# DeltaNet scan: where the next step's arguments and seeds stand between the two halves of the join, and the tails half a level later

## What is computed

```
a_mat = jnp.where(strict, jnp.einsum('bhncd,bhnsd->bhncs', kb, k) * decay, 0.0)
lhs = a_mat + jnp.eye(c_, dtype=a_mat.dtype)
rhs = jnp.concatenate([kb * jnp.exp(g_cum)[..., None], v * beta], axis=-1)
wu = lax.linalg.triangular_solve(lhs, rhs, left_side=True, lower=True)
...
v_new = u_i - jnp.einsum('bhcd,bhde->bhce', w_i, s)
s_new = s * jnp.exp(gl_i)[..., None, None] + jnp.einsum('bhcd,bhce->bhde', kt_i, v_new)
...
o_i = jnp.einsum('bhcd,bhde->bhce', qd_i, s) + jnp.einsum('bhcs,bhse->bhce', qk_i, v_new)
```

## Time and profile before

| | |
|---|---|
| median of 3 runs | 3947.25 us (3944.8 to 3965.12) |
| the profiled execution's own time | 3948.46 us |
| its span | 3946.6 us |
| mean granted clock of TensorE over the span | 0.952 |
| busy in the span: PE, DVE, ACT, POOL | 3696.8, 1920.1, 1100.5, 990.2 us |

### The profile page before, as it was taken

How to read it: one execution, slowest core, us unless ns; L and a number is a source line. 1 busy time by engine, 2 the same in 40 slices (tenths; PEclk the granted TensorE clock), 3 DMA queues, 4 the chain that set the end, 5 groups by cost and what they waited for, 6 DMA issues and landing times.

```text
span 3946.6 us, 78512 instructions
## 1 busy us (share of the span) xinstructions
PE 3696.8 (94%) x33918; PEld 3059.9 (78%) x33918; DVE 1920.1 (49%) x3377; ACT 1100.5 (28%) x2490; POOL 990.2 (25%) x731
## 2 busy tenths in 40 slices
PE   6999999888899999999998999999889899999997
PEld 5668888677788888888886668888677678888885
DVE  3455556444555333333357455556354554434445
ACT  3444243343312111011114453252343230001111
POOL 1000100144104333323223000100254043434341
PEclk8999999888799999999999999999797899999998
DMA  4240000100001010101111220000100111111111
GB/s 184 88 170 33 22 23 22 60 4 4 23 33 43 33 43 32 43 32 42 43 41 56 84 108 23 23 12 22 50 4 4 44 42 49 48 49 46 51 45 54
DMA packets 30530, 180.54 MB, mean 46 GB/s; under 512 B 2592, under 2 KB 8224, under 8 KB 15136
## 3 DMA queue, kind: packets, MB, share of 16 engines
q1 hardware_dynamic: 28944, 173.66, 11.8%
q10 hardware_dynamic: 1296, 2.61, 0.2%
HBM read 167.87 MB, written 8.39 MB: 45 GB/s over the span
## 4 chain that ended last, share of the span: by engine, by line
PE 84%; DVE 8%; ACT 5%; issue 2%; POOL 1%; DMA 1%; ACTq 0%; DVEq 0%; POOLq 0%; SPq 0%
PE ps L1401 38%; PE ps L801 9%; PE ps L811 8%; PE ps L836 4%; PE ps L934 4%; PE ps L976 2%; PE ps L1264 2%; PE ps L1273 2%; PE ps L1240 2%; PE ps L1328 1%; PE ps L1301 1%; PE ps L1019 1%; PE ps L1354 1%; PE ps L1041 1%; PE ps L845 1%
## 5 line engine op out<-in xcount | busy, mean ns | idle before, releaser
L1401 PE MATMUL ps<-Yn_parts,ring_parts 128*128 128x512 f32 (+1 forms) x3888 | 799.0, 367 | 2.4 <-DVE Yn_parts L2670 2.1
L1401 PEld LDWEIGHTS ps<-Yn_parts,ring_parts 128*128 128x128 f32 x3888 | 671.3, 189 | 126.7 <-DVE Yn_parts L2670 5.4
L1401 PE MATMUL ps<-temp_parts,ring_parts 128*128 128x512 f32 (+1 forms) x2560 | 726.3, 369 | 5.0 <-DVE Hn_parts L2611 3.6
L2930 POOL TENSOR_TENSOR ring_parts<-ring,consts 128x2048 fp32r<-128x2048 f32 x62 | 286.5, 4621 | 1154.5 <-DMA ring<-in_ff 1154.5
L1401 PEld LDWEIGHTS ps<-temp_parts,ring_parts 128*128 128x128 f32 x2560 | 464.9, 189 | 87.9 <-DVE Hn_parts L2611 4.1
L2558 DVE SCALAR_TENSOR_TENSOR Xn<-ps,mods,Xn 128x256 f32<-128x256 f32 (+1 forms) x364 | 251.8, 692 | 574.7 <-PE ps L1401 504.1
L801 PE MATMUL ps<-ring_parts,Xn_parts 128*128 128x256 f32 x2560 | 504.1, 292 | 24.1 <-DVE Hn_parts L2169 16.2
L1401 PE MATMUL ps<-Hn_parts,ring_parts 128*128 128x512 f32 (+1 forms) x1280 | 471.4, 368 | 0.0
L801 PEld LDWEIGHTS ps<-ring_parts,Xn_parts 128*128 128x128 f32 x2560 | 416.8, 195 | 27.2 <-issue 22.6
L1973 ACT ACTIVATE Yn<-ps 128x256 f32<-128x256 f32 (+1 forms) x160 | 88.6, 554 | 1237.8 <-PE ps L1401 1237.8
L2669 DVE TENSOR_TENSOR Yn<-Yn 128x256 f32<-128x256 f32 (+1 forms) x160 | 182.8, 1143 | 402.6 <-ACT Yn_parts L1975 402.6
(11 more groups left out here) (331 smaller groups left out, 5192.3 us busy)
## 6 DMA issues: line engine op xcount, KB each, us to landing
ring<-in_ff SPq DMA_DIRECT2D x64, 1024.0 KB, 4.7
ring<-in_ada SPq DMA_DIRECT2D x22, 2048.0 KB, 8.8
ring<-in_halves SPq DMA_DIRECT2D x28, 1024.0 KB, 4.8
Xn<-in_x SPq DMA_DIRECT2D x1, 5120.0 KB, 16.7
Hn<-in_ada SPq DMA_DIRECT2D x2, 2048.0 KB, 20.7
Xn<-in_x SPq DMA_DIRECT2D x2, 2048.0 KB, 18.2
kept_x<-Xn SPq DMA_DIRECT2D x4, 1024.0 KB, 4.0
Xn<-kept_x SPq DMA_DIRECT2D x1, 4096.0 KB, 14.8
```

The costliest lines, as they stand in the source:

```text
L1401: m = pe.matmul(ps[:, bank, 0:hi - lo], w[a][:, k, j * P:(j + 1) * P], x[b][:, k, lo:hi], start=(k == 0 and part == 0), stop=(k == k_n - 1 ...
L2930: link(TT(by(half_hi[s]), by(half[s]), spread(ones, 1, HALF // P), ALU.mult))
```

## The change

The list of the plan is written in another order, and what this needs is added:

- `arg` of q = 0 of the step after the next moves from behind `b` to between `a` and `b`; its `exp`, `gram` and `at` move into the first two levels of the next step. Both `seed`s and `start`s of the next step stand ahead of `b` on TensorE, and the first level stands directly behind `b`.
- `x1`, `off`, `x2` and `tail` of the step before move half a level later. `qkd` and `at` of q = 1 move to the last level. GpSimd's part of `reach` is an entry of its own, `rest`, behind `atm`.
- `lower` exists twice, for even and odd steps, and lies in `Yn`. `start` waits for the `a` of two steps ago.
- `b` writes to bank 0 (before: bank 3), behind the seed of the next step in the same bank, and starts no new sum there except in the last step. The wait for the copied inverse goes from `y` of level 1, q = 1, to `u` of level 1, q = 0.

The number of products, copies and additions is the same.

```diff
-            plan += one("gsum", 1, 0) + part("arg", 1, 0) + one("exp", 1, 0)
-            plan += both("start", 0) + both("seed", 0) + one("gram", 1, 0) + part("at", 1, 0) + both("kept", 0) + both("kt", 0)
+            plan += one("gsum", 1, 0) + part("arg", 1, 0)
+            plan += both("start", 0) + both("seed", 0) + both("kept", 0) + both("kt", 0)
...
-                plan += y(1) + late("x1", 0) + late("x1", 1) + soon("qkd", 0) + soon("mask", 0)
-                plan += u(1) + late("off", 0) + late("off", 1) + soon("pk", 0)
-                plan += y(2) + late("x2", 0) + soon("gsum", 1) + late("x2", 1) + soon("atm", 0)
-                plan += u(2) + part("arg", s_ + 1, 1) + late("tail", 0) + soon("exp", 1)
-                plan += y(3) + soon("gram", 1) + late("tail", 1)
-                plan += u(3) + part("at", s_ + 1, 1)
-                plan += y(4) + soon("qkd", 1) + late("acc", 0) + late("acc", 1) + one("reach", s_, 0)
-                plan += u(4) + soon("pk", 1) + one("reach", s_, 1) + soon("atm", 1)
-                plan += [("a", s_, 0, 0)] + both("wide", s_) + soon("start", 0) + then("gsum", 0)
-                plan += [("b", s_, 0, 0)] + soon("seed", 0) + soon("start", 1) + soon("mask", 1) + soon("seed", 1)
-                plan += part("arg", s_ + 2, 0) + then("exp", 0) + then("gram", 0) + part("at", s_ + 2, 0)
+                plan += y(1) + soon("exp", 0) + soon("gram", 0)
+                plan += u(1) + late("x1", 0) + late("x1", 1) + part("at", s_ + 1, 0)
+                plan += y(2) + late("off", 0) + late("off", 1) + soon("qkd", 0) + soon("mask", 0)
+                plan += u(2) + soon("pk", 0) + late("x2", 0) + soon("gsum", 1) + late("x2", 1) + soon("atm", 0)
+                plan += part("arg", s_ + 1, 1, (0, 1)) + y(3) + part("arg", s_ + 1, 1, (2, 3)) + late("tail", 0)
+                plan += u(3) + soon("exp", 1) + soon("gram", 1) + late("tail", 1) + late("acc", 0) + late("acc", 1)
+                plan += y(4) + part("at", s_ + 1, 1) + one("reach", s_, 0) + soon("start", 0)
+                plan += u(4) + soon("qkd", 1) + soon("pk", 1) + soon("atm", 1) + one("rest", s_, 0) + one("reach", s_, 1) + one("rest", s_, 1)
+                plan += [("a", s_, 0, 0)] + then("gsum", 0) + soon("seed", 0) + soon("start", 1) + both("wide", s_) + part("arg", s_ + 2, 0)
+                plan += soon("seed", 1) + [("b", s_, 0, 0)] + soon("mask", 1)
...
-                            if s_ and q == 1:
-                                pe.wait_ge(sems["u_inv0"], nth("u_inv0", 2 * s_))
-                                pe.wait_ge(sems["u_inv1"], nth("u_inv1", s_))
...
+                        if lv == 1 and q == 0 and s_:
+                            pe.wait_ge(sems["u_inv0"], nth("u_inv0", 2 * s_))
+                            pe.wait_ge(sems["u_inv1"], nth("u_inv1", s_))
...
+                        if s_ + 1 < NT:
+                            pe.wait_ge(sems["u_umm0"], nth("u_umm0", 5 * s_ + 6))
...
-                                    m = pe.matmul(ps[near, 3, of32(h, P)], sc[0]["step"][far, h, :], sc[q_]["upper"][far, h, :],
-                                                  start=True, stop=True, skip_group_check=True)
+                                    m = pe.matmul(ps[near, 0, of32(h, P)], sc[0]["step"][far, h, :], sc[q_]["upper"][far, h, :],
+                                                  start=(s_ + 1 == NT), stop=True, skip_group_check=True)
...
-                        if s_:
-                            dve.wait_ge(sems["u_lmm0"], nth("u_lmm0", 2 * s_ - 1))
-                        dve.transpose(flat(b["lower"]), b["atm"][s_ % 2][:, 0, :]).then_inc(sems[f"u_start{q}"], tally(f"u_start{q}"))
+                        if s_ >= 2:
+                            dve.wait_ge(sems["u_lmm0"], nth("u_lmm0", 2 * s_ - 3))
+                        dve.transpose(flat(b["lower"][s_ % 2]), b["atm"][s_ % 2][:, 0, :]).then_inc(sems[f"u_start{q}"], tally(f"u_start{q}"))
...
-                    if what == "reach":
+                    if what == "rest":
                         pool.wait_ge(sems[f"u_tv{q}"], nth(f"u_tv{q}", 4 * s_ + 1))
```

More of the change, by code:

```diff
@@ L401, in build @@
             b = {}
-            for n_ in ("lower", "upper", "step", "pk"):
+            for n_ in ("upper", "step", "pk"):
                 b[n_], r0_ = cut(ringf, r0_, H, 32)
+            b["lower"] = []
+            for _ in range(2):
+                half_, y0 = cut(Yn, y0, H, 32)
+                b["lower"].append(half_)
             b["inv"], r0_ = cut(ringf, r0_, H, 64)
@@ L1251, in dn_scan @@
                         for r in blocks32:
-                            m = pe.matmul(pair[r, 0:P], ident[r, r], b["lower"][r].rearrange("p h c -> p (h c)"), start=True, stop=False, skip_group_check=True)
+                            m = pe.matmul(pair[r, 0:P], ident[r, r], b["lower"][s_ % 2][r].rearrange("p h c -> p (h c)"), start=True, stop=False, skip_group_check=True)
                         m.then_inc(sems[f"u_umm{q}"], tally(f"u_umm{q}"))
@@ L1263, in dn_scan @@
                             for r in blocks32:
-                                m = pe.matmul(prod[r, of32(h)], atm[r, lv, of32(h)], b["lower"][r, h, :], start=True, stop=True, skip_group_check=True)
+                                m = pe.matmul(prod[r, of32(h)], atm[r, lv, of32(h)], b["lower"][s_ % 2][r, h, :], start=True, stop=True, skip_group_check=True)
                         m.then_inc(sems[f"u_ymm{q}"], tally(f"u_ymm{q}"))
@@ L1281, in dn_scan @@
                                     m = pe.matmul(ps[far, 2, of32(h, P)], sc[q_]["at"][s_ % kept_back(q_)][near, h, far],
-                                                  sc[q_]["lower"][near, h, :], start=True, stop=True, skip_group_check=True)
+                                                  sc[q_]["lower"][s_ % 2][near, h, :], start=True, stop=True, skip_group_check=True)
                         m.then_inc(sems["u_lmm0"], tally("u_lmm0"))
@@ L1872, in dn_scan @@
                         act.wait_ge(sems[f"u_umm{q}"], nth(f"u_umm{q}", 5 * s_ + lv + 1))
-                        A(flat(b["lower"]), ps[:, q, 0:P], ACT.Copy).then_inc(sems[f"u_lower{q}"], tally(f"u_lower{q}"))
+                        A(flat(b["lower"][s_ % 2]), ps[:, q, 0:P], ACT.Copy).then_inc(sems[f"u_lower{q}"], tally(f"u_lower{q}"))
                     if what == "a":
@@ L1883, in dn_scan @@
                                 near, far = blocks32[n_], blocks32[f_ % 2]
-                                m = A(sc[q_]["inv"][near, :, far], hd32(ps[near, 3, P:2 * P]), ACT.Copy)
+                                m = A(sc[q_]["inv"][near, :, far], hd32(ps[near, 0, P:2 * P]), ACT.Copy)
                             m.then_inc(sems[f"u_inv{q_}"], tally(f"u_inv{q_}"))
@@ L2495, in dn_scan @@
                         dve.wait_ge(sems[f"u_staged{q}"], nth(f"u_staged{q}", 2 * s_ + 1))
-                        if s_:
-                            dve.wait_ge(sems["u_lmm0"], nth("u_lmm0", 2 * s_ - 1))
-                        dve.transpose(flat(b["lower"]), b["atm"][s_ % 2][:, 0, :]).then_inc(sems[f"u_start{q}"], tally(f"u_start{q}"))
+                        if s_ >= 2:
+                            dve.wait_ge(sems["u_lmm0"], nth("u_lmm0", 2 * s_ - 3))
+                        dve.transpose(flat(b["lower"][s_ % 2]), b["atm"][s_ % 2][:, 0, :]).then_inc(sems[f"u_start{q}"], tally(f"u_start{q}"))
                     if what == "u":
                         dve.wait_ge(sems[f"u_lower{q}"], nth(f"u_lower{q}", 4 * s_ + lv))
-                        dve.transpose(flat(b["upper"]), flat(b["lower"])).then_inc(sems[f"u_upper{q}"], tally(f"u_upper{q}"))
+                        dve.transpose(flat(b["upper"]), flat(b["lower"][s_ % 2])).then_inc(sems[f"u_upper{q}"], tally(f"u_upper{q}"))
                     if what == "wide":
```

## The result

The changed kernel takes 3980.65 us (median of 12 runs, 3959.6 to 3999.98), beside 3954.56 us of the kernel before on the same chip (12 runs, 3944.71 to 3972.41). The ratio is 1.0058, 95% interval 1.0036 to 1.0079: it is slower, by 26 us between the medians and 23 us by the ratio, and outside of the predicted range.

The account below looks back on a forecast made before the run. TensorE's join waits and half clock were taken to bound the scans. Join -27.7, pk 1 +24.8, pk 0 +7.2, issue -5.4 (together -1) and clock -23 made -24 on 3948.46: 3924.5, as a median 3923; range 3890 to 3965 us.

Parts of the forecast that it names:

- Join, -27.7: From a to gram: TensorE's waits at seeds and gram go, 1.54 us a step, -27.7 us over 18 steps.
- pk 1, +24.8: Before pk of q = 1: TensorE newly waits for VectorE's qkd, 1.7 us at full clock, 0.1 at half; +24.8 us.
- pk 0, +7.2: Before pk of q = 0: TensorE waits for the later qkd, 0.5 us at full clock, none at half; +7.2 us.
- Moved at no cost: Later x1, off, x2, tails, and GpSimd's rest: TensorE filler or the join covers each, so 0 us.
- Issue gaps, -5.4: TensorE's instruction gaps before y and u: 0.3 us a step hidden by VectorE's lateness at pk; -5.4 us.
- Rival 3: Dense b, y, gram, u behind the join gain issue gaps, 18 x 1 us above forecast: 3941 us; chance 0.07.
- Clock, -23: Both scans: TensorE's half-clock time drops from 155 to 85 us as falls at joins lessen; -23 us, ends 0 and 50 back.
- 0.33: Both scans: assumed price of half clock, about a third of a us lost per us spent at it.
- Rival 4: New waits at pk hold the clock down from x1 to the tail of q = 1: 3980 to 4007 us; chance 0.13.

Follow-up runs that it names:

- e4: The changed kernel with x1, off, x2, the tails and the preparation between them at their old places, only the join changed: 3942.92 us, ratio 0.9982 to the kernel before.
- e1: The changed kernel with four extra 128x128 products, result not read, in front of pk of q = 1: 3968.13 us, ratio 1.0033 to the kernel before.
- e3: The changed kernel with VectorE's qkd of q = 1 moved back to directly behind at, ahead of reach 0: 3955.89 us, ratio 1.0005 to the kernel before.
- e2: The changed kernel with four extra 128x128 products, result not read, behind u of level 1: 3937.82 us, ratio 0.9955 to the kernel before.
- e5: The changed kernel with three extra products of 32x32 by 384 columns, result not read, behind u of level 1: 3990.66 us, ratio 1.0080 to the kernel before.
- e14b: The changed kernel with four extra 128x128 products, result not read, behind u of level 3: 3998.64 us, ratio 1.0118 to the kernel before.
- e9: The kernel before with x1, off, x2 and the tails half a level later, its join unchanged: 3965.95 us, ratio 1.0011 to the kernel before.

## Why the prediction was wrong, point by point

- *Join, -27.7: right.* The waits of seeds and gram were 26.8 us over both scans and are 0.8 now. The mechanism and the place are as they were put. *Falls before:* the prediction has 11 at joins and five in the middle of steps; the trace has four of the latter. More important, it took the falls at joins as one kind, while five long ones held 106 of the 126 us.
- *pk 1, +24.8: right.* 1.54 us at full clock where 1.7 was said, and 23.3 us in all. *pk 0, +7.2: too high.* It waits 7 times in 18 steps, at most 0.6 us, 3.3 us in all. Steps at full clock came out at 22.8 to 23.0 us, as forecast.
- *Moved at no cost: nearly.* y's copy (L1875) now makes u(1) wait for 1.3 us once in each scan, which the prediction hadn't. But "at no cost" looked at waits alone, and e4 shows that in the new join the late tails cost 30 to 38 us.
- *Issue gaps, -5.4: wrong sign.* They went from 18.5 to 29.0 us, +10.5. They weren't hidden by the wait at pk 1, as that term had it; they grew in the stretch that had become dense, and not "always" in 32x32 products: 3.1 us of them stand in off (L1318). Rival 3 has this mechanism, with 18 us where 10.5 were measured; its mark, over 15 us a scan, was reached in the first (15.4), missed in the second (13.6).
- *Clock, -23: the step that failed, and with it the forecast.* The prediction took 155 us down to 85; it went up to 215. That is +20 us at 0.33, 43 us away from the term. Its argument was that "nothing there keeps the clock down", about the surroundings of the two new waits. This was even right: e1 and e3 show that the wait at pk 1 does little to the clock, and pk 0 waits for longer in e2 (6.9 us) than in after, with the clock up. What it took at nothing is a fall where no wait for another engine is. It did say that falls might "move into the middle of a step", as the lower end of this term, and priced only waits as their cause. The falls left the join, 11 down to 2, as forecast, and 12 came 8.1 to 10.6 us behind "a", 160 us in all. Of the 54 us between -24 and +30 the clock is 43 and issue 16, while pk came out 5 lower than forecast.
- *Rival 4* has the size (slower, decides from 215 us at half clock on, the 3980 us of its lower case), and what it says of the half clock from x1 to tail 1, which doesn't bring the clock back, fits the trace. But its cause, a fall at the wait of pk 0 or pk 1, is not the one that the runs show, but for the four short falls near pk 1, 14 us of the 215. It was given 0.13.

The account closes: waits of the join and "b" -27 (with 0.8 left), pk +26.6, u(1) +2.6, issue +10.5, clock +20, together +33 us; measured +30.2 in the steps. The price of a third fits here; in e2, where 10 us stayed open, 0.40 would close the sum. Estimated by the Trainium skill's rule ("TensorE: Matmul & The Clock Gate", Part 1, HAM oscillation), by which time at half clock costs a half, the clock's share would be 30 us and the account 43: too high here too.

What the runs show of the cause is this: most of the clock is lost in the dense stretch of 32x32 and 64x64 products behind the join; full-size products there keep it (e2), thin ones don't (e5), full-size ones elsewhere hardly do (e14b). What stays open is why the late tails bring this about with the new join and not with the old one. In e9 13 falls stand at the joins, ten of them of 3.4 us, and seven others follow 10.3 to 16.1 us behind "a", three of which last 10.2 to 20.5 us; yet its total is hardly worse than before's. No run tells what makes this difference.

## What to carry to other kernels

Where a trace shows half clock, sum it as its own term, list the places of the falls by their distance from a landmark of the loop, and expect a denser order to move them: where a pause is removed, falls can come back in a stretch in which TensorE waits for no other engine. Try each move of a reordering alone before judging the whole: here one of them, the arguments between the halves of the join, was worth -0.84%, and the rest took more than that back. Add up the length of the falls and don't only count them. A wait that is removed may be worth several times its length (8.6 us of waiting, 32 us of time) or less than nothing, by what the clock does.

## What the runs showed of the hardware that was not expected

- Added work can pay. Four more 128x128 products a step, 1.08 us, made the kernel 43 us faster at one place (e2) and 18 us slower at another (e14b). At a third, where they fill a wait (e1), they gained 12 us, which the intervals don't tell from nothing.
- The clock can fall where TensorE isn't idle. In e5 it fell behind 6.7 us of 32x32 and 64x64 products without a gap, and with 7.6 us of gaps of issue in both scans 191 us are at half clock all the same. In after, the fall at 890 us has 2.33 us of gaps ahead of it; the others of its kind have 1.1 to 2.7 us in the 6.8 us from 2.7 us behind "a" on.
- The gaps of issue have their place by the count of TensorE's instructions. If one numbers all instructions that the trace has for TensorE (products, weight loads and those of its sequencer), all 506 such gaps in the scans of the 16 traces, from 0.2 to 1.8 us long, stand at the same remainder by 256 within one scan, give or take two. Not each 256th shows a gap: 30 of 102 before, 34 in after, 36 in e3 and 12 in e5, whose three long thin products take some 2 us of each step. So a gap moves when instructions are added or taken away ahead of it.
